# Moving a mean-removal product from the output of a recurrence to its values

## The reference

```
sa = S a ;  S = S * w + sa b^T + v k^T ;  y = S r
mu = mean(y);  var = mean((y - mu)^2)          # over the 64 channels of the head
yn = (y - mu) * rsqrt(var + eps) * gn_g + gn_b
out = yn + sum(r * k * r_k) * v                # the "bonus"
```

## Time and profile before

| | us |
|---|---|
| median of three runs | 3863.41 |
| lowest and highest run | 3861.2, 3867.28 |
| the profiled execution, its own time | 3858.04 |
| its span from the first to the last instruction | 3856.2 |

### The profile page before, as it was taken

How to read it: one execution, slowest core, us unless ns; L and a number is a source line. 1 busy time by engine, 2 the same in 40 slices (tenths; PEclk the granted TensorE clock), 3 DMA queues, 4 the chain that set the end, 5 groups by cost and what they waited for, 6 DMA issues and landing times. The chain is left out here.

```text
span 3856.2 us, 71009 instructions
## 1 busy us (share of the span) xinstructions
PE 3547.2 (92%) x31292; PEld 2932.6 (76%) x31292; DVE 2038.4 (53%) x3564; ACT 1541.8 (40%) x2599; POOL 250.7 (6%) x295
## 2 busy tenths in 40 slices
PE   6788989999898998989999799989999999999998
PEld 3566666766666676768888789847989799999877
DVE  1454454544455447774665556655444555555444
ACT  2333343333333333454544444425443444444433
POOL 0001111011111112002000000010000000000000
PEclk9899999999999999999999799999999999999999
DMA  9423323242333416443325354414553555555554
GB/s 379 144 70 97 112 86 117 70 128 84 117 101 97 128 44 234 151 138 113 109 91 185 128 164 136 154 61 155 184 181 125 175 175 175 182 180 185 190 182 163
DMA packets 349473, 548.57 MB, mean 142 GB/s; under 512 B 11724, under 2 KB 119916, under 8 KB 346988
## 3 DMA queue, kind: packets, MB, share of 16 engines
q1 hardware_dynamic: 346716, 538.78, 42.9%
q10 hardware_dynamic: 2448, 5.24, 0.4%
HBM read 535.86 MB, written 8.13 MB: 141 GB/s over the span
## 5 line engine op out<-in xcount | busy, mean ns | idle before, releaser
L302 PE MATMUL lane<-r,r 128*128 128x256 f32 (+1 forms) x8520 | 1506.9, 326 | 50.4 <-DVE r L260 40.4
L260 DVE TENSOR_TENSOR r<-ring,r 128x1024 fp32r<-128x1024 f32 x770 | 941.2, 1229 | 944.9 <-ACT r L299 943.6
L302 PEld LDWEIGHTS lane<-r,r 128*128 128x128 f32 x8520 | 1279.5, 193 | 207.7 <-DVE r L260 45.7
L302 PE MATMUL bank<-r,r 128*128 128x512 f32 (+2 forms) x6360 | 1402.2, 359 | 36.3 <-DVE r L260 24.8
L302 PEld LDWEIGHTS bank<-r,r 128*128 128x128 f32 x6360 | 1055.0, 195 | 241.9 <-issue 52.2
L299 ACT ACTIVATE r<-ring 128x1024 fp32r<-128x1024 f32 x770 | 808.8, 1056 | 957.1 <-PE lane L302 570.9
L302 PE MATMUL lane<-arena 64*64 64x64 f32 (+4 forms) x12940 | 622.6, 254 | 68.3 <-DVE arena L260 23.9
L302 PEld LDWEIGHTS lane<-arena 64*64 64x64 f32 (+3 forms) x12940 | 468.7, 140 | 234.2 <-issue 111.1
L299 ACT ACTIVATE arena<-lane 128x256 f32<-128x256 f32 (+3 forms) x578 | 248.8, 451 | 558.5 <-PE lane L302 446.4
L260 DVE TENSOR_TENSOR arena<-arena 128x256 f32<-128x256 f32 (+7 forms) x568 | 255.6, 481 | 35.8 <-ACT arena L299 14.9
L271 DVE COPY arena<-lane 128x256 f32<-128x256 f32 (+3 forms) x366 | 131.8, 362 | 267.2 <-PE lane L302 249.6
(11 more groups left out here) (94 smaller groups left out, 1252.2 us busy)
## 6 DMA issues: line engine op xcount, KB each, us to landing
ring<-in_w_gate_up SPq DMA_DIRECT2D x88, 1024.0 KB, 5.0
ring<-in_mod_w SPq DMA_DIRECT2D x73, 1024.0 KB, 5.2
ring<-in_ev_w_in SPq DMA_DIRECT2D x44, 1024.0 KB, 8.4
ring<-in_w_down SPq DMA_DIRECT2D x44, 1024.0 KB, 5.0
ring<-in_od_w_in SPq DMA_DIRECT2D x40, 1024.0 KB, 5.1
ring<-in_w_in SPq DMA_DIRECT2D x40, 1024.0 KB, 5.1
ring<-in_w_xkv SPq DMA_DIRECT2D x32, 1024.0 KB, 5.3
ring<-in_ev_w_out SPq DMA_DIRECT2D x28, 1024.0 KB, 5.2
```

Of the source, the lines that this page charges most:

```text
L260: return Nothing() if self.e is None else self.e.tensor_tensor(o, a, b, op)
L302: return Nothing() if self.e is None else self.e.matmul(o, l, r, start=start, stop=stop)
```

## The change

`turn_AV` no longer transposes v: it multiplies v as the stationary operand by `cen_bd` as the moving one, which gives v with tokens on the partitions and its mean removed. It does so ahead of the wait for A. The centring product of y and the copy of y are gone, and with them the second filling of the bank: y stays in columns 256 to 511 of `by` until read_out. ScalarE squares it from there in the step centre, where PE now does nothing. The bonus product goes into columns 0 to 255 of `by`, in the step gn_sum behind the sums of squares, and VectorE's multiplication by v moves from centre to gn_sum and waits for that product. One piece of filling moves from centre to gn_sum.

```diff
-        "QY": 1, ..., "centre": 3, "gn_sum": 6, "read_out": 2}
+        "QY": 1, ..., "centre": 2, "gn_sum": 7, "read_out": 2}
 # unit
-        b = bank(t)
-        step("centre", d, n, by, b)
+        step("centre", d, n, by)
         b2 = bank(pair_turns[d][0])
-        step("gn_sum", d, n, b, b2)
-        step("read_out", d, n, b, b2)
+        step("gn_sum", d, n, by, b2)
+        step("read_out", d, n, by, b2)
 # TensorE
     def turn_AV(d, n, b):
         s = M.lane[d]
-        turn4(b, [s.AR[:, 0, 0, :], s.AR[:, 1, 0, :], s.v[:, 0:P], s.v[:, P:2 * P]], ("v", d, n), ("A", d, n))
+        fresh(b)
+        pe.wait_ge(*at("v", d, n))
+        for c in range(2):
+            pe.mm(M.bank[b[0]][:, 256 + c * P:256 + c * P + P], s.v[:, c * P:c * P + P], C("cen_bd"), True, True)
+        pe.wait_ge(*at("A", d, n))
+        for c in range(2):
+            i = pe.tr(M.bank[b[0]][:, c * P:c * P + P], s.AR[:, c, 0, :], ident)
+        i.then_inc(*pe.n(("full", *b)))
-    def centre(d, n, by, b):
-        fresh(b)
-        pe.wait_ge(*at("y", d, n))
-        pe.mm(M.bank[b[0]][:, 0:256], C("cen_bd"), s.y, True, True)
-        pe.wait_ge(*at("rk", d, n))
-        pe.mm(M.bank[b[0]][:, 256:512], C("ones_bd"), s.t1, True, True).then_inc(*pe.n(("full", *b)))
-    def gn_sum(d, n, b, b2):
+    def gn_sum(d, n, by, b2):
         pe.wait_ge(*at("gn_sq", d, n))
         head_sums(b2, M.lane[d].ysq, C("head_mean"), "gn_sum", d, n)
+        pe.wait_ge(*at("rk", d, n))
+        pe.mm(M.bank[by[0]][:, 0:256], C("ones_bd"), M.lane[d].t1, True, True).then_inc(*pe.n(("bonus_mm", d, n)))
 # VectorE
-    def centre(d, n, by, b):
-        full(b)
-        v.wait_ge(*at("gn_sq", d, n))
-        v.tt(s.t1, M.bank[b[0]][:, 256:512], s.v, MUL).then_inc(*v.n(("bonus", d, n)))
+    def gn_sum(d, n, by, b2):
+        v.wait_ge(*at("bonus_mm", d, n))
+        v.tt(s.t1, M.bank[by[0]][:, 0:256], s.v, MUL).then_inc(*v.n(("bonus", d, n)))
 # VectorE, read_out
-        v.tt(s.yc, s.yc, M.bank[b[0]][:, 0:256], MUL).then_inc(*v.n(("free", *b)))
+        v.wait_ge(*at("y_mm", d, n, 3))
+        v.tt(s.yc, s.yc, M.bank[by[0]][:, 256:512], MUL).then_inc(*v.n(("free", *by)))
 # ScalarE
-    def state(d, n, i, by, bs):
-        if i == 3:
-            a.wait_ge(*at("y_mm", d, n, 3))
-            a.act(s.y, M.bank[by[0]][:, 256:512], ACT.Copy).then_inc(*a.n(("free", *by), ("y", d, n)))
-    def centre(d, n, by, b):
-        full(b)
-        a.act(s.ysq, M.bank[b[0]][:, 0:256], ACT.Square).then_inc(*a.n(("gn_sq", d, n)))
+    def centre(d, n, by):
+        a.wait_ge(*at("y_mm", d, n, 3))
+        a.act(M.lane[d].ysq, M.bank[by[0]][:, 256:512], ACT.Square).then_inc(*a.n(("gn_sq", d, n)))
```

More of the change, by code:

```diff
@@ L25 @@
 FILL = {"shift": 4, "kk_sum": 6, "keys": 4.5, "turn_AV": 2, "P_LR": 1, "KR0": 1, "KR1": 1, "solve": 0.5, "GH": 1,
-        "QY": 1, "state0": 2, "state1": 2, "state2": 2, "state3": 2, "centre": 3, "gn_sum": 6, "read_out": 2}
+        "QY": 1, "state0": 2, "state1": 2, "state2": 2, "state3": 2, "centre": 2, "gn_sum": 7, "read_out": 2}
 MOD_SHARE = 0.125
@@ L415, in __init__ @@
         self.G, self.DI, self.Q = q(2048), q(2304), q(2560)
-        self.y, self.yc, self.ysq = q(2816), q(3072), q(3328)
+        self.yc, self.ysq = q(3072), q(3328)
 class Pair:
@@ L1846, in state, with read_out @@
         m.then_inc(*pe.n(("y_mm", d, n, i)))
-    def centre(d, n, by, b):
-        s = M.lane[d]
-        fresh(b)
-        pe.wait_ge(*at("y", d, n))
-        pe.mm(M.bank[b[0]][:, 0:256], C("cen_bd"), s.y, True, True)
-        pe.wait_ge(*at("rk", d, n))
-        pe.mm(M.bank[b[0]][:, 256:512], C("ones_bd"), s.t1, True, True).then_inc(*pe.n(("full", *b)))
-    def gn_sum(d, n, b, b2):
+    def gn_sum(d, n, by, b2):
         pe.wait_ge(*at("gn_sq", d, n))
         head_sums(b2, M.lane[d].ysq, C("head_mean"), "gn_sum", d, n)
-    def read_out(d, n, b, b2):
+        pe.wait_ge(*at("rk", d, n))
+        pe.mm(M.bank[by[0]][:, 0:256], C("ones_bd"), M.lane[d].t1, True, True).then_inc(*pe.n(("bonus_mm", d, n)))
+    def read_out(d, n, by, b2):
         pe.wait_ge(*at("gn_rs", d, n))
@@ L2155, in tensor_program @@
         start, mod, mod_col, ev_times, lora, kk_sum, keys, turn_AV, P_LR, KR, double, KV,
-        turn_BK, solve, QY, GH, state, centre, gn_sum, read_out,
+        turn_BK, solve, QY, GH, state, gn_sum, read_out,
         combine, first_done, times_w, pool_mix, pool_done, gate_row, lat_done, ctx_done, h1, h1_done, v_rows, k_turned, q_turned,
@@ L3054, in vector_program @@
     take = {f.__name__: f for f in (
-        start, mod_col, h0, ev_split, lora_shift, gate_in, shift, kk_sum, keys, P_LR, KR, double, solve, QY, GH, state, centre,
+        start, mod_col, h0, ev_split, lora_shift, gate_in, shift, kk_sum, keys, P_LR, KR, double, solve, QY, GH, state, gn_sum,
         read_out, combine, first_done, split_w, split, pool, pool_mix, pool_done, gate_diag, add_first, ctx_done,
@@ L3661, in scalar_program @@
     take = {f.__name__: f for f in (
-        start, mod_row, h0, ev_split, lora_in, lora_shift, rkv_in, gate_in, shift, kk_sum, gn_sum, state, turn_AV, double, KV, turn_BK, solve, centre, read_out,
+        start, mod_row, h0, ev_split, lora_in, lora_shift, rkv_in, gate_in, shift, kk_sum, gn_sum, turn_AV, double, KV, turn_BK, solve, centre, read_out,
         combine, spill_out, first_done, split_w, pool, pool_done, gate_row, norm0_q, h1, h1_done, to_q, to_k, to_v,
```

## The result

The changed kernel takes 3854.4 us (median of ten runs), the kernel before, run beside it, 3864.7 us (ten runs): a ratio of 0.9968, 95% interval 0.9959 to 0.9977, or 10.3 us less by the medians. One of the ten runs of the changed kernel was disturbed and is left out of the ratio (the median of the nine others is 3854.1). The profiled execution of the changed kernel took 3848.7 us with a span of 3846.9. The prediction was 3851.6, 11.8 us less than before.

What follows compares the result with a forecast made beforehand. PE sets the pace in the 32 units, busy 1157 of 1283 us. The terms -13.8 + 2.6 - 0.9 - 0.5 + 0.8 = -11.8 us take 3863.4 to 3851.6 us; range 3844 to 3861 us, chance 0.61.

Steps and rivals of the forecast that it cites:

- The centring product, -13.8: In centre, one of two 0.43 us products goes in each of 32 units, with no wait around it: 13.8 us less.
- turn_AV, +2.6: Two products replace two transpositions, 0.23 us more; 16 units pay, 6 gain 0.21 in waits, 10 count zero: 2.6 us more.
- The bonus behind gn_sum, -0.9: In units 4 and 12 lane 1's 0.43 us bonus product runs inside the next unit's kk_sum wait: 0.9 us less.
- The last unit, -0.5: Without the centre pair and the 0.41 us wait for the square, gn_sum comes 1.3 us earlier; 0.5 us less counted here.
- Unit 11, +0.8: In lane 0 the moved filling piece ends a projection sum, leaving a new wait at read_out: about 0.8 us more.
- Only the bare work counts: Rival: hidden work comes back in the next wait, 6.4 us less 0.8 stays, 3857.8 us; bare work or less, chance 0.26.
- VectorE's queue: Rival: VectorE, held 1.6 us in gn_sum, delays remainders PE needs; once in each of 16 rounds, 3877 us; chance 0.05.
- Four transpositions: Rival: in turn_AV a product costs four transpositions, 0.63 us more in 16 units; 3.2 us less in all, 3860 us; chance 0.05.

Runs made afterwards that it cites:

- e1: The changed kernel with the filling of centre and gn_sum back as before (3 and 6 pieces): 3848.7 us, ratio 0.9968.
- e5: The changed kernel with ScalarE's square in the step state 3, where the copy stood, instead of in centre: 3851.9 us, ratio 0.9980.
- e8: The changed kernel with the filling back (3 and 6) and ScalarE's square in the step state 3: 3851.1 us, ratio 0.9973.

## Why the prediction was right, point by point

The value held: 11.8 us forecast, 10.3 and 11.5 measured. The two large steps of the sum held too, the small ones did not all, and one thing that it took for fixed moves by as much as a term: the clock. That its two parts, 5.1 us lost in the units and 2.7 gained behind them, largely cancel in the changed kernel is luck, and the small terms that were off are too small to move the sum out of its interval.

- **The centring product, -13.8.** Right. The doubled product shows the same 13.8 us of busy time, 0.41 to 0.43 us in each place, without a wait, and 14.6 us more work in the table. The two kernels without the product and with the old turn_AV have 13.8 us less work than before. In the medians they stand at -11.2 (-7.3 to -17.0) and, with the filling back, at -17.0 (-10.0 to -22.4), against a sum of -15.2 for the second.
- **turn_AV, +2.6.** The mechanism held, and the size within what the traces can tell. The price lies between 0.21 (work) and 0.30 us (from neighbour to neighbour, all steps) where 0.23 was taken; what the pitch inside a run of seven records left out is the longer distance behind the first record of a group. The hiding is as described, with one thing that I had not seen: PE waits for v, which VectorE forms just ahead of A, so the products hide because A takes VectorE another 0.42 us (v's products begin 0.4 us ahead of A's end and take 0.54, so 0.15 us stick out). The wait fell from 18.8 and 21.7 us to 13.7 and 12.4. Against the two kernels with the old turn_AV the changed kernel and e1 have 7.5 and 7.2 us more work and 5.5 us less idle time: about +2 us. Alone on the kernel before the step measured +8.7 and +11.3, which its trace puts to the clock and not to the step.
- **The bonus behind gn_sum, -0.9.** Smaller than forecast, as far as the rows show. The two waits of the earlier trace rows in which it was to run, 3.31 and 4.19 us before (3.45 and 4.15 in the second trace), should be 0.43 us shorter each; they are 0.16 and 0.31 us shorter in the changed kernel, where two executions of before differ by up to 0.14. No total can resolve it.

```profile
552.79 0.61 PE L302 MATMUL lane<-cm,arena 128*128 128x2 f32 x4 [3.15 <-ACT arena L299]
1219.72 0.80 PE L302 MATMUL lane<-cm,arena 128*128 128x2 f32 x4 [3.88 <-ACT arena L299]
```

- **The last unit, -0.5.** Wrong in its mechanism. The square did not stay ahead of PE; in ScalarE's queue it stands behind a copy that waits for PE, and a wait of 0.41 us became 1.27 us. The sums were to come 1.3 us earlier and come no earlier (2.99 us behind the small matmuls in both kernels), and to the last row the unit gained 0.1 us (0.4 between the second traces of both) and not 1.36 (the 0.5 and the 0.86 of two centring products). Moving the square removed this wait and gained nothing, since ScalarE's queue holds up the roots as well.
- **Unit 11, +0.8.** The wait is there, 0.66 us in both executions, and gone with the filling back. In the totals the filling's place is worth 2 us beside the changed kernel (-13.5 to -11.5, across chips) and 0.2 us with the square moved (-10.5 to -10.3): not told from zero.
- **What I took as fixed.** "Untouched by the change" was true of the instructions behind the units and not of their time. That part takes 2399 us in the changed kernel, 2402 in the kernel before, and up to 2409 in others. By the means of two traces each the span fell by 11.1 us, 7.6 in the units and 3.5 behind them. In the units PE's work fell by 5.7 us (6.8 on the mean of all seven traces with these instructions; 7 forecast) and its idle time by 7.1 (4 to 5 forecast), which is 12.8 us against the 11.8 of the sum; PE was busy at 1.2 GHz for 10.3 us more, and that gave 5.1 us back. Behind the units it was busy at 1.2 GHz for 5.4 us less, a gain of 2.7. My sum had no term for either. PE's idle time differs by up to 4.9 us between two executions of one kernel, so the terms below 5 us are not confirmed to the microsecond.

**The rivals.** *Only the bare work counts* gave 3857.8: what is hidden would come back in the next wait, so that PE's idle time would not fall. It fell, from 124.6 and 129.5 us to 121.2 and 118.8, and to 116.3 to 119.2 in e1, e5 and e8; the intervals of the changed kernel's medians (8.9 and 6.2 us less at the least, 5.6 by this rival) speak against it too, but less, since the clock is in them. *VectorE's queue* is out: the waits that it foretold did not come (PE waits 5.6 and 5.1 us for VectorE's 128x1024 remainders, 5.4 and 6.1 before), and taking the hold away did not make the kernel faster. *Four transpositions* is out: the new products take 0.54 us for two of them with the first record's delay, and the same four records without it would take 0.45, where four transpositions take 0.43 and eight 0.87. The rule of the Trainium skill, "TensorE: Matmul & The Clock Gate", Terms, that the transposing mode is four times faster for FP32, does not hold for this shape: the factor is about two.

What stays open: what sets the granted clock, in the units and behind them, and whether the change has a part in it; and which instruction makes PE wait longer when the bonus is held until read_out.

## What to carry to other kernels

Price a step by the time from the record before it to the record behind it, with the same neighbours, and not by the pitch inside a long run: the first record of a group had up to 0.1 us of its own here. Take the steps without a wait and at one clock level apart from the others. When work leaves a path with no wait around it, its busy time is its worth; when it stands ahead of a wait, look at which input of the step comes first and put there what needs only that. Before a difference of 0.2% is put down to an edit, split the trace at the edit and see whether the untouched part kept its time, and take the engine's time at the lower clock out of its busy time: that repeated within 2.3 us here where the end of the edited part moved by 5.3.

## What the runs showed that I had not expected

The part of the program behind the units, with the same 13,732 records of PE, takes from 2398.6 to 2409.3 us depending on the kernel ahead of it, and repeats within 1.5 us for the same kernel. It goes with how long the clock stands at 1.2 GHz there (125 to 130 us against 140 to 154 us). One place is the stretch of 1000 records from about 2430 to 2675 us: 241 to 243 us long at 20 to 27 us of lower clock in seven traces, and 246 us at 37.5 us of it in the other seven. PE's work behind the units, with half of its time at 1.2 GHz taken off, is the same within 1.4 us in all fourteen, so by this estimate the longer time at the lower clock accounts for the longer part. What makes it fall there was not tested: no kernel moved that part alone.
